# Trainium2, one core: the entry of a mixture-of-experts loop rebuilt (norm sums on VectorE, slot lists by one-hot matmuls, scratch buffers moved)

## What is computed

```python
x = x + g1 * (merged @ w_out[l])                        # end of the mixer
h = rmsnorm(x, norm_ffn_g[l]) * (1.0 + sc2) + sh2
scores = sigmoid(h @ router_w)                          # 64 experts
_, idx = top_k(scores + router_bias, 6)
gsel = scores[idx] / sum(scores[idx]) * 2.5
y = swiglu(h, w_shared_gu, w_shared_down)               # shared expert, width 256
for every expert e:                                     # width 256
    y[tokens of e] += gate * swiglu(h[tokens of e], w_exp_gu[e], w_exp_down[e])
x = x + g2 * y
```

## Time and profile before

| | us |
|---|---|
| median of three runs | 3215.95 (3207.77 to 3219.42) |
| the profiled execution, its own time | 3210.36 |
| its span, first to last instruction | 3208.7 |
| TensorE busy | 2916.7 (91%) |
| VectorE busy | 2033.4 (63%) |
| ScalarE busy | 1568.6 (49%) |
| GpSimd busy | 611.6 (19%) |

### The profile page before, as it was taken

How to read it: one execution, slowest core, us unless ns; L and a number is a source line. 1 busy time by engine, 2 the same in 40 slices (tenths; PEclk the granted TensorE clock), 3 DMA queues, 4 the chain that set the end, 5 groups by cost and what they waited for, 6 DMA issues and landing times. The chain is left out here.

```text
span 3208.7 us, 42356 instructions
## 1 busy us (share of the span) xinstructions
PE 2916.7 (91%) x13756; PEld 2217.9 (69%) x13756; DVE 2033.4 (63%) x2871; ACT 1568.6 (49%) x2422; POOL 611.6 (19%) x577
## 2 busy tenths in 40 slices
PE   5899998899879999999579999989998899999993
PEld 4577776677667777777456777756776677777773
DVE  4544446454468888888645444555545788888885
ACT  2342423432347777777233334243223677777770
POOL 0100000100133333333210000000003233333332
PEclk9899999999789999999669999999998899999995
DMA  7124332233469999999412243312324799999975
GB/s 227 55 86 144 105 131 79 84 111 119 154 242 362 364 368 370 359 360 351 192 52 73 92 144 111 131 60 86 129 100 192 289 367 358 362 371 365 357 260 207
DMA packets 119333, 671.67 MB, mean 209 GB/s; under 512 B 27468, under 2 KB 28876, under 8 KB 84204
## 3 DMA queue, kind: packets, MB, share of 16 engines
q1 hardware_dynamic: 85792, 605.91, 50.7%
q0 software_dynamic: 31456, 57.70, 5.5%
q10 hardware_dynamic: 1932, 6.16, 0.8%
HBM read 656.86 MB, written 55.02 MB: 222 GB/s over the span
## 5 line engine op out<-in xcount | busy, mean ns | idle before, releaser
L1831 DVE TENSOR_TENSOR ew_lo<-ew,e_hi 128x2048 fp32r<-128x2048 f32 x260 | 595.8, 2292 | 191.9 <-ACT e_hi L1689 191.7
L690 PE MATMUL bank<-h_hi,w_hi 128*128 128x512 f32 x1248 | 514.5, 412 | 50.9 <-DVE w_lo L624 19.3
L1689 ACT ACTIVATE e_hi<-ew 128x2048 fp32r<-128x2048 f32 x260 | 497.5, 1914 | 105.4 <-PE bank L1976 81.5
L624 DVE TENSOR_TENSOR w_lo<-raw,w_hi 128x1024 fp32r<-128x1024 f32 x198 | 242.7, 1226 | 439.4 <-ACT w_hi L616 439.2
L690 PE MATMUL bank<-h_hi,w_lo 128*128 128x512 f32 x1248 | 503.1, 403 | 0.0
L690 PE MATMUL bank<-h_lo,w_hi 128*128 128x512 f32 x1248 | 500.8, 401 | 0.0
L1976 PE MATMUL bank<-e_hi,x_hi 128*128 128x512 f32 x1040 | 419.7, 404 | 0.0
L1976 PE MATMUL bank<-ew_lo,x_hi 128*128 128x512 f32 x1040 | 408.7, 393 | 0.0
L1976 PE MATMUL bank<-e_hi,x_lo 128*128 128x512 f32 x1040 | 406.5, 391 | 0.0
L616 ACT ACTIVATE w_hi<-raw 128x1024 fp32r<-128x1024 f32 x198 | 208.2, 1052 | 283.6 <-DMA raw<-in_wmix 184.3
L1591 POOL DMA_INDIRECT y_d<-y,idx x128 | 219.1, 1712 | 624.1 <-issue 527.0
(11 more groups left out here) (289 smaller groups left out, 4454.1 us busy)
## 6 DMA issues: line engine op xcount, KB each, us to landing
ew<-in_wexp SPq DMA_DIRECT2D x130, 2048.0 KB, 9.7
raw<-in_wmix SPq DMA_DIRECT2D x297, 512.0 KB, 4.0
ew<-in_wexp SPq DMA_DIRECT2D x130, 1024.0 KB, 9.4
yt<-y_d SPq DMA_DIRECT2D x8, 3072.0 KB, 15.6
ada0a<-in_ada SPq DMA_DIRECT2D x2, 2048.0 KB, 13.5
ada0b<-in_ada SPq DMA_DIRECT2D x2, 2048.0 KB, 22.3
h_d<-htok ACTq DMA_DIRECT2D x8, 512.0 KB, 2.7
xg<-h_d,idx POOLq DMA_INDIRECT x130, 9.4
```

What stands on the lines that cost most here:

```text
L624: nc.vector.tensor_tensor(w_lo[q % SPLIT][:], raw[u % RAW][:], w_hi[q % SPLIT][:].bitcast(F32), ALU.subtract).then_inc(lo_done, 1)
L690: ins = nc.tensor.matmul(out, lhs, rhs, start=start, stop=stop)
L1689: nc.scalar.activation(e_hi[h][:], up_part(ew, j, h), ACT.Copy).then_inc(whi_done, 1)
L1831: nc.vector.tensor_tensor(up_part(ew_lo, j, h), up_part(ew, j, h), e_hi[h][:].bitcast(F32), ALU.subtract).then_inc(wlo_done, 1)
```

## The change

- **Norm.** ScalarE squares each piece of xT behind its `out` job in the mixer block; VectorE adds the eight squares into one buffer `pr[2]`; four one-column matmuls stand in place of 32. Mean and root are in the mixer block too.
- **Order at the entry.** VectorE scales all eight pieces first; ScalarE adds the shift (semaphore `hf_ready`, on which the logits now wait); the high and low parts are made among the routing steps. The sigmoid's table is loaded ahead by a small activation. The shared jobs 0 and 1 stand before the rank matmuls, 2 and 3 behind them, 4 to 9 behind the slot lists, 10 and 11 behind the transposes of expert 0.
- **Slot lists.** GpSimd makes `filed` (one-hot times row number, one-hot times gate, two products of 128x1536). VectorE makes `at_slot` (one-hot of the slot, 128x768 per group of 128 tokens, four of them). TensorE sums 24 products of 128x128 by 128x128 in f32 into a PSUM bank: row number and gate of each slot of each expert. Six VectorE instructions write that to `slots`. The 24 indirect writes to `slot_d` stay (they are read for overflow blocks alone), one in each of the loop's first 24 steps on GpSimd. Reading back and clearing `xg` go.
- **Scratch.** `onehot`, `filed`, `ohmul`, `at_slot` lie over hf and htok; ew2's load waits for nothing of the routing. `e_hi`, `x_hi`, `x_lo` lie in h's buffers, so expert 0's weights are split from shared job 3 on.
- **Early weights.** The first three shared tiles and the 512 KB initialization of `slot_d` are issued in the mixer block.
- **Spacing of y.** `y_d` has 8 rows per token in place of 6 (row 8t+k, six used), so that the token is the row number shifted right by 3.

The diff, cut to its core:

```diff
-        y_d = nc.dram_tensor("y_d", [S * TOPK, D], F32, kind="Internal").ap()
+        y_d = nc.dram_tensor("y_d", [S * YROWS, D], F32, kind="Internal").ap()
...
@@ mixer block, SyncE @@
-                    for u in range(RAW, MIX_TILES):
+                    for u in range(RAW, MIX_TILES + RAW):
                         load_tile(sp, l, u)
+                        if u == MIX_TILES // 2:
+                            sp.dma_start(slot_d, skip_d).then_inc(slot_init, 16)
@@ mixer block, ScalarE, VectorE, TensorE @@
+                    def square_out(act, k):
+                        wait_out_of(act, "x", k)
+                        if k >= 3:
+                            act.wait_ge(xs_used, k - 2)
+                        nc.scalar.activation(sn[k % 2][:] if k else pr[2][:], xT[:, k, :], ACT.Square).then_inc(xs_ready, 1)
...
+                    def add_square(k):
+                        dve.wait_ge(xs_ready, k + 1)
+                        if k >= 2:
+                            dve.wait_ge(xs_used, k - 1)
+                        nc.vector.tensor_tensor(pr[2][:], pr[2][:], sn[k % 2][:], ALU.add).then_inc(xs_used, 1)
...
+                    pe.wait_ge(xs_used, KD - 1)
+                    for t in range(TC):
+                        ins = nc.tensor.matmul(MB[:, t:t + 1], pr[2][:, t * P:(t + 1) * P], ones[:, 0:1], start=True, stop=True)
@@ expert block, SyncE @@
-                    sp.dma_start(slot_d, skip_d).then_inc(slot_init, 16)
-                    for u in range(MIX_TILES, MIX_TILES + 3):
-                        load_tile(sp, l, u)
...
                     load_up(1, 1)
                     load_down(1, 1)
-                    sp.wait_ge(dest_ready, 1)
+                    load_tile(sp, l, MIX_TILES + RAW)
                     load_up(2, 2)
                     load_down(2, 2)
+                    for u in range(MIX_TILES + RAW + 1, NTILES):
+                        load_tile(sp, l, u)
@@ expert block, GpSimd @@
+                        if isinstance(it, int) and it < NPAIR // 8:
+                            slot_row_out(8 * it + j)
...
-                    for i in range(4):
-                        ins = nc.gpsimd.memset(xg[i][:], 0.0)
-                    ins.then_inc(pchain, 1)
-                    pool.wait_ge(slot_out, 16 * NPAIR)
-                    pool.dma_start(slots[:], slot_rows[0:BLK]).then_inc(slots_in, 16)
+                    pool.wait_ge(oh_ready, 1)
+                    pool.wait_ge(h2_out[0], 32)
+                    nc.gpsimd.tensor_tensor(filed[:, :, 0, :], onehot[:], yrow[:].unsqueeze(2).broadcast_to([P, NPAIR, NE]),
+                                            ALU.mult).then_inc(filed_ready, 1)
+                    pool.wait_ge(gates_ready, 1)
+                    nc.gpsimd.tensor_tensor(filed[:, :, 1, :].rearrange("p (t k) e -> p t k e", t=TC), oh,
+                                            biased[:].unsqueeze(2).broadcast_to(four), ALU.mult).then_inc(filed_ready, 1)
+                    pool.wait_ge(slots_set, 1)
@@ expert block, ScalarE @@
+                    high(0, 3)
+                    act.wait_ge(logits_ready, 1)
+                    nc.scalar.activation(sgt[0:NE, :], OB[0:NE, :], ACT.Sigmoid).then_inc(score_ready, 1)
+                    high(3, 4)
+                    rows(0)
+                    high(4, 6)
+                    rows(1)
+                    high(6, KD)
+                    rows(2)
+                    rows(3)
...
-                    act.wait_ge(mark, shared_mark)
+                    act.wait_ge(mark, up_mark)
@@ expert block, VectorE, the order after onehot @@
+                    weights_low(1)
...
+                    job_out(1)
+                    dve.wait_ge(rank_ready, 1)
+                    link(dve, nc.vector.tensor_tensor(om, oh, rank.unsqueeze(2).broadcast_to(four), ALU.mult))
+                    product_low(0)
+                    link(dve, nc.vector.tensor_reduce(destf[:], ohmul[:], AX.X, ALU.add))
+                    weights_low(2)
+                    file_slots(0)
+                    file_slots(1)
+                    weights_low(3)
+                    job_out(3)
+                    dve.wait_ge(filed_ready, 2)
+                    link(dve, nc.vector.tensor_reduce(gsel[:].rearrange("p t k -> p (t k)"), filed[:, :, 1, :], AX.X, ALU.add))
+                    file_slots(2)
+                    product_low(1)
+                    file_slots(3)
...
+                    weights_low(4)
+                    dve.wait_ge(slots_full, TC)
...
@@ expert block, TensorE @@
+                    shared_job(2)
+                    shared_job(3)
+                    pe.wait_ge(filed_ready, 2)
+                    for i in range(NPAIR):
+                        if i % TOPK == 0:
+                            pe.wait_ge(at_slot_ready, i // TOPK + 1)
+                        ins = nc.tensor.matmul(OB[:, 0:2 * NE], at_slot[i // TOPK % 2][:, i % TOPK, :], filed[:, i, :, :].rearrange("p a e -> p (a e)"),
+                                               start=i == 0, stop=i == NPAIR - 1)
+                        if i % TOPK == TOPK - 1:
+                            ins.then_inc(slots_full, 1)
...
                     transposes(0, 0, 0)
-                    for j in range(4):
+                    shared_job(10)
+                    shared_job(11)
+                    step(0, 0, first=True)
+                    list_blocks()
+                    for j in range(1, 4):
                         step(0, j, first=True)
```

270 lines of the change are left out of this document (175 added, 95 removed).

## The result

The changed kernel takes **3186.37 us** (median of 4 runs, 3183.81 to 3187.34) beside 3212.62 us of the kernel before in the same session (3207.77 to 3219.42; the three runs known ahead of the prediction and a fourth, 3209.29): ratio **0.9918**, 95% interval 0.9904 to 0.9932. It is faster, by 26 us. The forecast was 3155 us with a range of 3138 to 3184, so it gained less than half of what was forecast, and 2 us less than the range allowed.

The account below looks back on a forecast made before the run. TensorE bounds the loop; at each layer's entry it stands idle in a chain. Gains of 30.4 and 28.7 us, together 59, take 3210.36 to 3151; the runs' median gives 3157, put at 3155 us, range 3138 to 3184.

Parts of the forecast that it names:

- Norm: Entry, last `out` step to first `hf`: eight sums stay of 64, first `hf` at 823.3 where it was 834.56, 11.2 us gained.
- barrier to the next block 0.3: End of the mixer block, behind the root: passing to the expert block costs 0.3 us.
- Logits: Entry, TensorE after scaling and shifts: 16 instructions at 0.43 us each (the low clock), done at 831.8 us.
- Stores to DRAM: Entry, before TensorE turns the token rows: a store lands in 2.7 to 6.6 us, middle taken; job 0 at 841.1 or 843.7.
- Early loading of ew2 brings nothing: Entry, SyncE's load of expert 2's weights: no row has a wait for it, so loading it early gains nothing.
- Jobs, one-hot, rank, slot lists: Entry, job 0 to expert 0's product: rank 3 us, slot sums 6.2 to 12 us; product at 888.3 with job 0 at 841.1.
- VectorE beside GpSimd: Entry, during GpSimd's two `filed` products: slowing of VectorE's chain could be 0 to 4 us per layer, taken as 0.
- In the loop: GpSimd's steps 0 to 23: 24 slot writes of 1.35 us fit in 2.8 us free per step and cost nothing.
- rival (d): Expert loop: slot writes hold GpSimd up, 48 at 1.35 us give back 65 us; 3220 us, no change; chance 0.03.
- Rival (b): Expert loop, steps 0 to 63: becomes DMA-bound and the kernel slower, 3270 us at 1 us more per step; chance 0.03.
- (a): Entry bound by VectorE and ScalarE, each late item delaying all behind it; 10 to 12 us per layer back, 3177; chance 0.20.
- (c): Adding back reads y slower: loads taking twice 7.2 us cost 29 us more per layer; 3213 us, no change; chance 0.03.

Follow-up runs that it names:

- experiment 2: The changed kernel with GpSimd's root of the norm at the start of the expert block instead of the mixer block's end: 3181.09 us, ratio 0.99.
- experiment 4: Changed kernel with GpSimd's root in the expert block and SyncE waiting for h's stores only ahead of the fourth shared tile and ew2: 3168.4 us.

## Why the prediction was wrong, and where it was right

**Direction and mechanism held.** The kernel is faster, the gain is in the entry, and each layer gives about the same. The entry reaches the forecast of about 73 us (71.0 us) once two costs that the prediction priced too low are taken out. The steps that failed are the block's end behind the root (0.3 us; 3.65 measured), the stores to DRAM (2.7 to 6.6 us; a median of 8.1), and the end of the expert block, which was put at nothing (5.65 us in each layer). The steps, in its order:

- **Norm.** Eight sums, 1.44 us (forecast 1.7), root's end 4.4 us after the last `out` step (forecast 4.3): right. Wrong was the step "barrier to the next block 0.3": that price was read where GpSimd had been done for 200 us. The prediction named the block's end as a new wait behind the root and put no price on GpSimd's own part of it. It is 4.42 us of DRAIN, 3.65 seen by TensorE; moving the root out of the block gave `hf` 3.0 to 3.2 us earlier and entries 3.1 and 4.0 us shorter.
- **Logits.** Forecast done 15.3 us after the last `out` step, measured 21.2 in layer 1. Of the 5.9 us 3.4 are the block's end and 0.8 the wait for `pay`. The other 1.7 are a misreading: "0.43 each (the low clock)" is what one of these matmuls takes at the high level. In the trace after, four start 0.87 us apart until 839.0, where the granted clock was 0.50, and the other twelve 0.43 apart at 1.00. So the lower bound's 3.4 us for logits at full clock was not there to be had.
- **Stores to DRAM.** This is the term that failed most. The bounds were 2.7 and 6.6 us and I took the middle; the median was 8.1 us. Job 0 came 35.2 and 37.3 us after the last `out` step and not 24.6 to 27.2. The window of the stores has a DMA share of 1.01, above the 0.90 by which the term was argued. The upper bound was taken from a scatter in the loop, a transfer that shares the engines with loads issued one at a time; here 5 MB were still to be moved when the first store was issued. The Trainium skill (DMA: Bandwidth & Descriptors, "Queues, rings and completion order") says that each DMA engine takes turns between the queues that have work, a packet at a time. The trace agrees, 121 packets against 106 and 117 against 116, and it shows what a prediction has to put in: the packets' sizes. With 4 KB against 16 KB a store gets a fifth of the window's 410 GB/s by that page, 82 GB/s, an estimate; the trace has 0.41 MB in 5 us, the same 82 GB/s. The 3.9 us to the first packet come on top and stay unexplained.
- **"Early loading of ew2 brings nothing"** was half the truth: nobody waits for it, so it cannot help, but it hurts. With ew2 and the tile ahead of it behind the stores, the kernel was 12.7 us faster than experiment 2's by the medians and by the entries. I had looked for who gains from an earlier transfer and not for who shares the engines with it.
- **Jobs, one-hot, rank, slot lists.** Job 0 to expert 0's product 47.6 and 46.9 us, forecast 47.2. The slot sums took 0.12 us per instruction, at the lower bound (5.9 us of 6.2 to 12), and the rank matmuls ran at full clock. `filed` took 2.77 and 3.48 us, below and at the lower bound.
- **VectorE beside GpSimd**, put at 0: `sel` took 2.99 where it took 2.75 us, nothing else shows. The Trainium skill's lock (SBUF — State Buffer, "Who interferes with whom") is between GpSimd and a VectorE instruction that reads both inputs from SBUF, at the same time. In the changed kernel none such ran beside the two `filed` products (beside them VectorE reduced or read PSUM, as forecast), so the trace shows no lock and doesn't test it.
- **In the loop.** The 48 slot writes cost TensorE 2.3 us in layer 1 (2.6 us of waits for gathered rows against 0.3 before), and the loop's length differs by 0.6: "cost nothing" is off by that much, with the rows one to a step. Packed they held GpSimd up as rival (d) said, for less than its 32 us per layer: the burst of 24 made TensorE wait 18.3 us and the loop 16 us longer. Rival (b) did not come: 149.92 of 150 us busy at share 0.98.
- **What was missing altogether** is the end of the expert block. The prediction followed the slot writes to the next gather and stopped there. They also lengthen GpSimd's DRAIN 400 us later, 5.65 us in each layer, 11.3 us of the 34.5 by which the profiled execution (3185.85 us) misses 3210.36 less 59. The entries are 20.8, the mixer blocks 1, the loops 1.

**Rivals.** (a) had 10 to 12 us per layer coming back at the entry, because a late item, "a store, a lock, low clock", delays all behind it; 10.4 came back. The late store is one of its items, and it did delay all three engines, so that half of (a) came true. The chain of VectorE and ScalarE by itself does not bind the entry: with the store and the block's end taken away it takes 71 us. Its 3177 us would have been near, had the DRAIN not been added. (c) is refuted in the kernel before alone; at the pitch of 32 KB the rate of y's loads did not change. The rule of the Trainium skill on large pitches (DMA: Bandwidth & Descriptors, "Latency and other measured facts") begins far above it, and nothing of it shows here.

## What to carry to other kernels

An edit that brings work forward must be priced also for what it now runs beside, in packets and their sizes and not only in bytes. Move a transfer that nobody waits for behind the short one that somebody does, and small tiles ahead of large weights. Work that is moved to the end of a block on an engine that was idle puts that engine's closing DRAIN on the path; look up its length in the trace before moving it. And transfers that are spread into a loop can be free in the loop and still be paid for at the block's end.

## What I had not expected of the hardware

- GpSimd's DRAIN at a block's end took 0.96 to 10.35 us with the same 154 indirect transfers in the block, repeatable within some 10 ns, set by where 24 small writes of 128 rows stand among 130 larger transfers. The mixer block's took 3.32 us with GpSimd idle for long, 4.42 right behind a 1.03 us instruction.
- A 512 KB store took 2.7 us alone and a median of 8.1 us (up to 12.8) where 5 MB of another engine's loads were still to be moved at the first store; where 0.9 MB were left (experiment 4), a median of 3.0 us. Queues take turns by packets: 117 packets of loads moved 1.72 MB while 116 of stores moved 0.41 MB.
- 24 indirect writes in one burst on GpSimd took 1.0 us each (mean 998 ns) with no gather in flight; behind four gathers, and with expert 0's transfers beside them, single ones took 2.3 to 4.3 us and the burst lasted 43 us (882.9 to 925.9) where 31 were expected.
